# A two-layer hybrid backbone kernel: fill products before TensorE's waits, the routing order, an earlier load of the Fourier matrices, tap norms as columns, and the first low parts moved

## The chip, the cores and the metric

The kernel runs on one NeuronCore of a Trainium2 chip. The metric is the device time of one execution in microseconds (us). The engines are named as in the profile: PE is TensorE's matmul side and PEld its weight loads, DVE is VectorE, ACT is ScalarE, POOL is GpSimd, SP is SyncE, which here only issues DMAs.

## The reference, cut to what matters

Two layers work on 256 latent tokens and 256 context tokens, each of 1024 channels, in float32.

```
for l in range(2):
    h  = modulate(rms_norm(x, norm_mix[l]), shift1, scale1)      # all tokens; l = 1: context for k, v only
    p  = h @ w_in[l]                # columns v, x1, x2 (Hyena), q, kv (attention), f (Fourier), three gates
    ya = attention(q, k, v)         # windowed, sink logits, keys of latents and context
    yf = real(fft2(f))              # per sequence of 256, per group of 128 channels
    yh = hyena(v, x1, x2)           # two long convolutions: DFT, times spectrum, inverse DFT
    # the spectra: taps = mlp(positions) * decay;  k = taps / sum(|taps|) over time, per channel
    x += g1 * ((sum of sigmoid(gate_b) * (y_b @ w_b)) @ w_out)
    h2 = modulate(rms_norm(x, norm_ffn[l]), shift2, scale2)
    aff = sigmoid(h2 @ w_router)    # 16 experts in 4 groups; best group, then its top 2
    x += g2 * sum over the token's 2 experts of weight * (silu(h2 @ Wg) * (h2 @ Wu)) @ Wd
out = rms_norm(x, norm_final)
```

Layer 1 carries on only the latent tokens: it has two blocks of 128 tokens where layer 0 has four.

## The kernel before

**Tiles.** Tokens stand in blocks of 128 (`T`, four in layer 0, two in layer 1). Products are of 128 rows by 512 columns into one of seven PSUM banks that go round (bank 7 is for the modulation). Large float32 products are made of three products of fp32r parts: ACT copies a weight quarter into its high part (`split_high`, L1020, or `high` for experts, L1252), DVE subtracts to get the low part (`split_low`, `low`, L1369), and PE runs high x high, high x low, low x high. Small products and transposes are plain float32.

**Order.** The five engines run five programs written out by hand and joined by semaphores. `plan_jobs(l)` lists every PSUM result of a layer in PE's order with the engine that takes it out ("act" or "dve"); on PE `begin(name)` waits until the bank's former result is taken, and on ACT and DVE `take(name)` waits for the product. Each engine runs strictly in its own order, so an instruction that waits holds up all that stand behind it.

**The opening.** `OPENING` interleaves the first modulation group (eight "units", each a 1 MB load and one set of products) with the making of layer 0's filter spectra in steps 0 to 7 (`filter_step`). Steps 2 and 3 make the taps and their absolute values, steps 4 and 6 the norm (`tap_norm`: PE sums over time with a matrix of ones, DVE takes the reciprocal, L1424), steps 5 and 7 the five spectra of an order (`tap_spectra`: PE, then one DVE multiply by `rnorm` each, L1369). Layer 1's steps run at the end of layer 0, PE's one after the other, DVE's between the two `combine` calls that add the experts' outputs to x.

**The rows.** `first_norm` modulates the rows of a block on DVE (`modulated`, L1495 and L1369), PE transposes them (`turn_row`, L2041), ACT takes the high part, DVE the low part (`low_rows`), and `project` multiplies by v's weights. In layer 0 DVE makes v's four low parts after the second row. Then x1, x2, q, kv and f follow, while SP stores and loads rows for the short convolution that DVE runs (`convolve`).

**Fourier, attention, Hyena.** The Fourier matrices (`four`, 640 KB) are loaded by POOL (L823) after the last convolution of the layer, since they lie where its stage rows lie. PE runs fp and fy (two products each), then attention, then for each order the spectra of u (eight products of 512 columns), DVE's ten multiplies, and the inverse products c behind this wait:

```
for s in range(nt // 2):
    pe.wait_ge(spec_ready, 2 * T_BEFORE[l] + 2 * (o * (nt // 2) + s + 1))
    for tt in range(2):
        b = begin("c", l, o, s, tt)
```

**Routing.** After w_out's products per block come the norm, the transposes of the new rows (hT), and the router products (`logits`: 8 products with 16 columns). ACT copies them, takes high parts of the first expert's first two weight quarters (`high(0, 0)`, `high(0, 1)`) between the last but one and the last block, and applies the sigmoid. DVE ranks (`ranked`), PE counts (`cnt`, `tot`), DVE makes the places of experts 0 and 1, and `place_first` on PE gathers expert 0's rows by products. Then the experts run, 12 weight quarters of 1 MB each.

Of the kernel before, what the change touches and what calls it, by code (L numbers as in the profile page):

```python
# [177 lines left out]
def filter_jobs(l, g):  # L178

    taps = [[("f3", l, o, sign, tt) for sign in (1, 0) for tt in range(2)] for o in range(2)]  # L180
    spec = [[("fk", l, o, b) for b in range(5)] for o in range(2)]
    return [[("fl", l, 1)], [("fl", l, 2)], taps[0], taps[1], [("fn", l, 0)], spec[0], [("fn", l, 1)], spec[1]][g]

# [18 lines left out]
def hybrid_kernel(nc, A, out):  # L202
    jobs = [(("fc",), "dve")]
    for kind, *what in OPENING:
        if kind == "filter":
            jobs += [(n, "dve") for n in filter_jobs(*what)]
    for l in range(DEPTH):
        for g in range(FILTER_STEPS if l else 0):
            jobs += [(n, "dve") for n in filter_jobs(l, g)]
# [49 lines left out]
    with ctx:  # L259
# [58 lines left out]
        rnorm = [mixed[:, 2560:3072], mixed[:, 5120:5632]]  # L318
# [9 lines left out]
        four = work[:, 0:1280]  # L328
# [142 lines left out]
        abs_ready = sem("abs_ready")  # L471
        hid_ready = sem("hid_ready")
# [280 lines left out]
        def _(pool):  # L753
# [65 lines left out]
            for l in range(DEPTH):  # L819
                T = tokens_of(l)  # L820
                Lb = NE * l
                pool.wait_ge(conv_done, 3 * (T_BEFORE[l] + len(T)))
                pool.dma_start(four, A["k_four"]).then_inc(four_loaded, 16)  # L823
# [138 lines left out]
        def _(act):  # L962
# [87 lines left out]
            def filter_step(l, g):  # L1050
# [4 lines left out]
                if g in (2, 3):  # L1055
                    o = g - 2
                    for sign in (1, 0):
                        for tt in range(2):
                            act.wait_ge(dve_took, TAKEN[("f3", l, o, sign, tt)])
                            nc.scalar.activation(filt_abs[l][o][sign][:, tt, :], filt_pm[l][o][:, sign, tt, :], ACT.Abs)\  # L1060
                                .then_inc(diff_abs, 1)

            for kind, *what in OPENING:
                if kind == "filter":
# [4 lines left out]
                    if what == [0, 7]:  # L1069
# [3 lines left out]
            for l in range(DEPTH):  # L1073
# [89 lines left out]
                for s in range(len(T) // 2):  # L1163
                    for g in range(5):
# [3 lines left out]
                        if g > 0:  # L1168
                            b = take(("fy", l, s, g - 1))
                            nc.scalar.activation(yfT[:, g - 1, s * SEQ:(s + 1) * SEQ], b[:, 0:SEQ], ACT.Copy)\  # L1170
# [90 lines left out]
                nc.scalar.activation(rt[:, 0, 0:len(T) * NE], rt[:, 0, 0:len(T) * NE], ACT.Sigmoid).then_inc(aff_ready, 1)  # L1261

# [82 lines left out]
                weigh(l, early_blocks(l), GOT_EARLY[l])  # L1345
# [5 lines left out]
        def _(dve):  # L1351
# [75 lines left out]
            def tap_spectra(l, o):  # L1427
# [1135 lines left out]
```

## Time and profile before

| what | value |
|---|---|
| median of three runs | 2232.47 us (2231.63 to 2233.43) |
| the profiled execution's own time | 2234.48 us |
| its span in the trace | 2232.9 us |
| PE busy | 2072.1 us (93%), 9594 matmuls |
| DVE busy | 1628.2 us (73%) |
| ACT busy | 1162.4 us (52%) |
| mean granted TensorE clock | 0.967 of full |

A granted clock of 1.00 is 2.4 GHz, 0.50 is 1.2 GHz. Every stage has its own bound, so shares of the whole span say little; the chain of waits and the windows of single stretches are to be read.

### The profile page before, as it was taken

The page shows a single profiled execution, that of the slowest core. Times are in us where ns is not written, and L with a number is a line of the kernel's source. Part 1 is how long each engine was busy: PE and PEld are TensorE (multiplying, and loading weights), DVE is VectorE, ACT ScalarE, POOL GpSimd, SP SyncE. Part 2 cuts the span into 40 slices and gives each one's busy share as a digit, 9 for nine tenths or more (in the row PEclk, how much of TensorE's full clock was granted, in tenths as well). Part 3 has the DMA queues.
Part 4 walks back from the last instruction along what each step waited for, and adds up shares of the span by engine and source line. Part 5 has one row for each costly group of instructions (what it writes and reads, how often), then busy time and mean ns, then how long its engine had stood idle before and what let it go on. Part 6 is the DMA issues. An engine that isn't in the chain of part 4 may idle for free.

```text
span 2232.9 us, 26104 instructions
## 1 busy us (share of the span) xinstructions
PE 2072.1 (93%) x9594; PEld 1606.3 (72%) x9594; DVE 1628.2 (73%) x1648; ACT 1162.4 (52%) x1121; POOL 186.8 (8%) x244
## 2 busy tenths in 40 slices
PE   6899999999989999999999797899889999999993
PEld 2687746666777888888887375567678888888882
DVE  4674681233657999999999876545669999999994
ACT  3223602122226777777776344234447777777772
POOL 2000000111003000000000200000110000000001
PEclk9999999999979999999999898999889999999997
DMA  9665006666358999999999566056579999999992
GB/s 343 216 227 203 11 5 226 234 234 223 131 198 294 375 398 388 398 395 386 406 389 385 212 226 238 8 206 227 212 279 373 381 402 394 390 403 387 395 396 106
DMA packets 131134, 630.75 MB, mean 282 GB/s; under 512 B 13677, under 2 KB 15865, under 8 KB 74860
## 3 DMA queue, kind: packets, MB, share of 16 engines
q1 hardware_dynamic: 101432, 505.23, 59.0%
q0 software_dynamic: 26704, 119.69, 14.3%
q10 hardware_dynamic: 2916, 4.73, 0.6%
q8 instruction: 53, 0.87, 0.2%
q14 instruction: 29, 0.24, 0.0%
HBM read 597.39 MB, written 32.20 MB: 282 GB/s over the span
## 4 chain that ended last, share of the span: by engine, by line
PE 82%; DVE 8%; DMA 4%; issue 3%; ACT 2%; SPq 1%; DVEq 0%; POOL 0%; ACTq 0%; POOLq 0%
PE bank L2036 76%; PE bank L2373 3%; DVE work L1369 2%; DVE ring L1369 2%; DMA work<-hp_dram 2%; PE bank L2058 2%; DMA ring<-in_w_mod_dram 1%; PE bank L2246 1%; DVE m_lo L1369 1%; PE bank L2041 1%; DVE mixed L1369 1%; ACT w_hi L1252 1%; DVE w_lo L1369 1%; ACT m_hi L1020 0%; DMA ring<-in_w_in_dram 0%
## 5 line engine op out<-in xcount | busy, mean ns | idle before, releaser
L1369 DVE TENSOR_TENSOR w_lo<-ring,w_hi 128x2048 fp32r<-128x2048 f32 x384 | 873.5, 2288 | 110.5 <-ACT w_hi L1252 110.2
L1252 ACT ACTIVATE w_hi<-ring 128x2048 fp32r<-128x2048 f32 x384 | 737.2, 1921 | 248.3 <-PE bank L2036 248.3
L2036 PE MATMUL bank<-w_hi,xsT_hi 128*128 128x512 f32 x1024 | 399.4, 390 | 6.5 <-DVE xsT_lo L1369 4.7
L2036 PE MATMUL bank<-w_lo,xsT_hi 128*128 128x512 f32 x1024 | 398.5, 389 | 0.0
L2036 PE MATMUL bank<-w_hi,xsT_lo 128*128 128x512 f32 x1024 | 315.3, 389 | 0.0
L1020 ACT ACTIVATE m_hi<-ring 128x1024 fp32r<-128x1024 f32 (+1 forms) x128 | 131.1, 1032 | 349.9 <-PE bank L2036 303.3
L1369 DVE TENSOR_TENSOR m_lo<-ring,m_hi 128x1024 fp32r<-128x1024 f32 (+1 forms) x128 | 150.9, 1190 | 208.4 <-ACT m_hi L1020 206.4
L2036 PE MATMUL bank<-m_hi,hT_hi 128*128 128x512 f32 (+1 forms) x640 | 250.5, 391 | 16.9 <-DVE m_lo L1369 4.8
L2036 PE MATMUL bank<-m_lo,hT_hi 128*128 128x512 f32 (+1 forms) x688 | 263.6, 383 | 0.0
L2036 PEld LDWEIGHTS bank<-w_hi,xsT_hi 128*128 128x128 f32 x1024 | 192.2, 188 | 48.7 <-DVE xsT_lo L1369 5.3
L2036 PE MATMUL bank<-m_hi,hT_lo 128*128 128x512 f32 (+1 forms) x592 | 225.3, 381 | 0.0
L2036 PEld LDWEIGHTS bank<-w_hi,xsT_lo 128*128 128x128 f32 x1024 | 192.2, 188 | 40.0
L2036 PEld LDWEIGHTS bank<-w_lo,xsT_hi 128*128 128x128 f32 x1024 | 192.2, 188 | 39.7
L2036 PE MATMUL bank<-w_hi,hexpT_hi 128*128 128x512 f32 x512 | 203.3, 397 | 5.8 <-issue 5.8
L2036 PE MATMUL bank<-w_lo,hexpT_hi 128*128 128x512 f32 x512 | 200.1, 391 | 0.0
L2036 PEld LDWEIGHTS bank<-m_hi,hT_hi 128*128 128x128 f32 x640 | 122.2, 191 | 65.7 <-issue 25.4
L2036 PE MATMUL bank<-w_hi,hexpT_lo 128*128 128x512 f32 x512 | 158.4, 391 | 0.0
L2036 PEld LDWEIGHTS bank<-m_lo,hT_hi 128*128 128x128 f32 x688 | 131.2, 191 | 23.4
L2036 PEld LDWEIGHTS bank<-m_hi,hT_lo 128*128 128x128 f32 x592 | 112.5, 190 | 21.8
L2036 PEld LDWEIGHTS bank<-w_hi,hexpT_hi 128*128 128x128 f32 x512 | 96.9, 189 | 26.2 <-issue 7.0
L2036 PEld LDWEIGHTS bank<-w_hi,hexpT_lo 128*128 128x128 f32 x512 | 96.4, 188 | 20.9
L2036 PEld LDWEIGHTS bank<-w_lo,hexpT_hi 128*128 128x128 f32 x512 | 96.7, 189 | 19.1
(240 smaller groups left out, 2256.3 us busy)
## 6 DMA issues: line engine op xcount, KB each, us to landing
ring<-in_w_exp_gate_dram SPq DMA_DIRECT2D x128, 1024.0 KB, 8.7
ring<-in_w_exp_up_dram SPq DMA_DIRECT2D x128, 1024.0 KB, 7.3
ring<-in_w_exp_down_dram SPq DMA_DIRECT2D x128, 1024.0 KB, 7.7
ring<-in_w_in_dram SPq DMA_DIRECT2D x44, 1024.0 KB, 5.9
work<-in_w_mod_dram POOLq DMA_DIRECT2D x40, 1024.0 KB, 6.2
ys_dram<-work POOLq DMA_DIRECT2D x32, 512.0 KB, 7.8
work<-hp_dram SPq DMA_DIRECT2D x54, 256.0 KB, 4.4
work<-mod_dram POOLq DMA_DIRECT2D x12, 1024.0 KB, 9.6
```

Of the source, the lines that this page charges most:

```text
L1020: nc.scalar.activation(high_of(key, q)[:, 0:n], ring[:, cols], ACT.Copy).then_inc(split_hi, 1)
L1252: nc.scalar.activation(w_hi[:, pos % N_SPLIT, :], raw(i), ACT.Copy).then_inc(hi_done, 1)
L1369: return nc.vector.tensor_tensor(o, a, b, op)
L2036: return nc.tensor.matmul(o, a, b, start=first, stop=last)
L2041: ins = nc.tensor.transpose(dst[:, j * P:(j + 1) * P], src[:, j * P:(j + 1) * P], ident)
L2058: ins = nc.tensor.matmul(bank[MOD_BANK][32 * j:32 * (j + 1), :], c_act[:, k, :], src[:, j * CH:(j + 1) * CH], start=k == 0, stop=k == KB - ...
L2246: ins = nc.tensor.matmul(b[at_d:at_d + HD, 0:P], vrow[:, k, g * HD:(g + 1) * HD], PT[:, (i - 3) % 2, g, n, :], start=n == 0, stop=n == len ...
L2373: ins = nc.tensor.transpose(dst[:, j * P:(j + 1) * P], s4[:, j // 2, j % 2, :], ident)
```

## The change

- `keep_busy(b, n)` issues n float32 products of the identity with 256 columns of the DFT matrix into a bank that the next job overwrites. It stands before waits of PE: 8 (layer 1: 14) before the first row of the first norm, 4 before v's first product in layer 0, 3 (layer 1: 6) and 2 before the router products of the last two blocks, 1 before the last h2 row, 12 (layer 1: 10) before `cnt`, 1 before `place_first`, and 8 before c in layer 1 alone. `begin` is moved ahead of these waits.
- The sum of absolute taps is made as columns: eight products with one column each, a reciprocal of 128x4, one multiply with the identity (`norm_at`), one product with ones that spreads it back over 512 columns (job "fr", behind the third spectrum), and a copy by ACT into `rnorm`. DVE waits for that copy before the first spectrum's multiply. At the end of layer 0 ACT's two `weigh` calls stand between these copies.
- In layer 0 v's high parts are made right after the first "fr" copy, and v's low parts one by one between the five multiplies of the first spectra.
- The Fourier matrices are loaded to another place after the last row transposes of the first norm, in two DMAs; ACT waits for the last convolution before the first `yfT` write.
- Routing: `high(0, 0)` goes before the last but one router copy, `high(0, 1)` behind the sigmoid; `low(0, 1)` goes behind `idx_tok`; the maximum of `tot` is taken earlier.

```diff
+def filter_taker(name):
+    return "act" if name[0] == "fr" else "dve"
...
+        norm_at = [[filt_abs[l][o][0][:, 0, :].rearrange("p (j n) -> p j n", j=4) for o in range(2)] for l in range(DEPTH)]
+        rcol = [mixed[:, at:at + 8].rearrange("p (o j) -> p o j", o=2) for at in (3300, 5120)]
...
-        four = work[:, 0:1280]
+        four, four_d = work[:, 3072:4096], work[:, 5632:5888]
...
+                pool.wait_ge(mm_done, DONE[("hT", l, 0, 3, 1)])
+                pool.dma_start(four_d, A["k_four"][:, 1024:1280]).then_inc(four_loaded, 16)
+                pool.dma_start(four, A["k_four"][:, 0:1024]).then_inc(four_loaded, 16)
                 pool.wait_ge(conv_done, 3 * (T_BEFORE[l] + len(T)))
-                pool.dma_start(four, A["k_four"]).then_inc(four_loaded, 16)
...
+                if g in (5, 7):
+                    o = g // 7
+                    b = take(("fr", l, o))
+                    nc.scalar.activation(rnorm[l][o], b[:, :], ACT.Copy).then_inc(act_took, 1)
...
-                    if what == [0, 7]:
+                    if what == [0, 5]:
                         for _ in split_high(("in", 0, "v")):
...
+                            if g == 1:
+                                act.wait_ge(conv_done, 3 * (T_BEFORE[l] + len(T)))
                             nc.scalar.activation(yfT[:, g - 1, s * SEQ:(s + 1) * SEQ], b[:, 0:SEQ], ACT.Copy)\
...
+                high(0, 0)
                 logits(l, T[-2])
-                high(0, 0)
-                high(0, 1)
                 transposed(l, T[-1])
                 logits(l, T[-1])
                 act.wait_ge(act_took, TAKEN[("r", l, T[-1])])
                 nc.scalar.activation(rt[:, 0, 0:len(T) * NE], ..., ACT.Sigmoid).then_inc(aff_ready, 1)
+                high(0, 1)
...
-                weigh(l, early_blocks(l), GOT_EARLY[l])
+                for i, tb in enumerate(early_blocks(l)):
+                    weigh(l, [tb], GOT_EARLY[l])
+                    if l + 1 < DEPTH:
+                        filter_step(l + 1, 5 + 2 * i)
...
             def tap_norm(l, o):
                 b = take(("fn", l, o))
-                nc.vector.reciprocal(rnorm[l], b[:, :]).then_inc(dve_took, 1)
+                nc.vector.reciprocal(rcol[l][:, o, :], b[:, 0:4]).then_inc(dve_took, 1)
                 dve.wait_ge(dve_took, took[0])
+                TT(norm_at[l][o], ident.unsqueeze(1).broadcast_to([P, 4, P]),
+                   rcol[l][:, o, :].unsqueeze(2).broadcast_to([P, 4, P]), ALU.mult).then_inc(norm_spread, 1)
+            def tap_spectra(l, o, beside=()):
+                dve.wait_ge(act_took, TAKEN[("fr", l, o)])
                 for k in range(5):
                     b = take(("fk", l, o, k))
-                    TT(made_spectra[l][:, o, k, :], b[:, :], rnorm[l], ALU.mult).then_inc(dve_took, 1)
+                    TT(made_spectra[l][:, o, k, :], b[:, :], rnorm[l][o], ALU.mult).then_inc(dve_took, 1)
                     dve.wait_ge(dve_took, took[0])
+                    for _ in beside:
+                        break
...
-                    filter_step(*what)
+                        tap_spectra(0, 0, split_low(("in", 0, "v")))
+                    else:
+                        filter_step(*what)
...
-                    if l == 0 and tb == 1:
-                        for _ in split_low(("in", 0, "v")):
-                            pass
...
                 low(0, 0)
-                low(0, 1)
                 dve.wait_ge(aff_ready, l + 1)
...
                         .then_inc(idx_ready, 1)
+                low(0, 1)
                 dve.wait_ge(second_mm, l + 1)
...
+            def keep_busy(b, n):
+                for _ in range(n):
+                    mm(b[:, 0:2 * P], ident, dft[:, 0, 0:2, :].rearrange("p b m -> p (b m)"), True, True)
...
-                for tt in range(2):
-                    ins = mm(b[:, :], ones, filt_abs[l][o][1][:, tt, :], tt == 0, tt == 1)
+                for j in range(4):
+                    for tt in range(2):
+                        ins = mm(b[:, j:j + 1], filt_abs[l][o][1][:, tt, j * P:(j + 1) * P], ones[:, 0:1], tt == 0, tt == 1)
...
+                    if k == 3:
+                        pe.wait_ge(norm_spread, 2 * l + o + 1)
+                        b = begin("fr", l, o)
+                        mm(b[:, :], ones, norm_at[l][o].rearrange("p j n -> p (j n)"), True, True).then_inc(mm_done, 1)
...
+                def fill_of(p, k):
+                    if p == 0 and k == 0:
+                        return 14 if l else 8
+                    return int(p == 1 and k == nt - 1)
                 def turn_row(p, k, tb, row):
-                    pe.wait_ge(rows_ready, ROWS_AT[l, p] + k + 1)
                     for half in range(2):
                         b = begin("hT", l, p, tb, half)
+                        if half == 0:
+                            keep_busy(b, fill_of(p, k))
+                            pe.wait_ge(rows_ready, ROWS_AT[l, p] + k + 1)
...
+                        b = begin(*name)
+                        if l == 0 and tb == 0:
+                            keep_busy(b, 4)
                         pe.wait_ge(dve_took, TAKEN[ready(tb)])
-                        b = begin(*name)
...
-                        pe.wait_ge(spec_ready, 2 * T_BEFORE[l] + 2 * (o * (nt // 2) + s + 1))
                         for tt in range(2):
                             b = begin("c", l, o, s, tt)
+                            if tt == 0:
+                                keep_busy(b, 8 if nt == 2 else 0)
+                                pe.wait_ge(spec_ready, 2 * T_BEFORE[l] + 2 * (o * (nt // 2) + s + 1))
...
+                    b = begin("r", l, tb)
+                    if tb in T[-2:]:
+                        keep_busy(b, 2 if tb == T[-1] else 3 if l == 0 else 6)
                     pe.wait_ge(act_took, TAKEN[("hT", l, 1, tb, 1)])
...
+                b = begin("cnt", l)
+                keep_busy(b, 12 if nt == 4 else 10)
                 pe.wait_ge(sel_ready, l + 1)
...
+                    keep_busy(bank[2], 1)
                     pe.wait_ge(placed, 2 * l + 1)
```

## Rows read from the trace of the kernel before

**Rows 1.** Chain of waits, opening: start us, length us, what.

```profile
43.60 19.08 PE bank L2036 x44
...
68.64 4.62 DVE m_lo L1369 x4
...
74.52 7.38 PE bank L2036 x24
...
82.77 5.49 PE bank L2036 x24
```

**Rows 2.** Timeline of DVE, opening and last h2 row: start us, us, instruction, idle before.

```profile
40.56 3.36 DVE L1424 RECIPROCAL mixed<-bank 128x512 f32<-128x512 f32 x1 [1.36 <-PE bank L2036]
...
45.84 0.18 DVE L1450 RECIPROCAL stat<-stat 128x4 f32<-128x4 f32 x1 [0.27 <-ACT stat L1001]
...
62.79 0.69 DVE L1369 TENSOR_TENSOR ring<-bank,mixed 128x512 f32<-128x512 f32 x1 [1.02 <-PE bank L2036]
...
642.88 1.22 DVE L1369 TENSOR_TENSOR mixed<-mixed,work 128x1024 f32<-128x1024 f32 x1
```

**Rows 3.** Timeline of PE: router products and transposes of layer 0, fy of layer 1.

```profile
637.20 1.85 PE L2036 MATMUL bank<-wr,hT 128*128 128x16 f32 x16
638.90 1.07 PE L2041 MATMUL bank<-const,mixed 128*128 128x128 f32 x8
641.66 3.59 PE L2036 MATMUL bank<-wr,hT 128*128 128x16 f32 x16 [1.69 <-ACT hT L1032]
...
1379.05 1.03 PE L2036 MATMUL bank<-ring,work 128*128 128x256 f32 x4
```

**Rows 4.** Chain of waits, routing of layer 0.

```profile
647.18 1.90 ACT w_hi L1252
...
650.10 3.61 PE bank L2036 x16
...
659.32 14.70 PE bank L2036 x88
```

**Rows 5.** Windows there: A:B length, busy PE PEld DVE ACT POOL, clock, DMA, GB/s.

```profile
662.60:669.30 6.70, 6.70 (x36) 6.70 (x35) 3.15 (x14) 0.00 (x0) 0.00 (x0) 0.56 0.00 0
669.30:674.00 4.70, 4.70 (x41) 4.52 (x39) 0.84 (x3) 0.60 (x1) 2.19 (x3) 1.00 0.18 61
```

**Rows 6.** Window before layer 1's first row.

```profile
1274.70:1282.90 8.20, 0.00 (x0) 0.00 (x1) 7.52 (x15) 0.20 (x1) 0.53 (x1) 0.79 0.70 291
```

**Rows 7.** Chain of waits, layer 1's first products.

```profile
1285.35 1.97 PE bank L2041 x8
1287.32 23.00 PE bank L2036 x96
```

**Rows 8.** Windows before and in the Fourier products of layer 1.

```profile
1365.20:1372.60 7.40, 0.00 (x1) 0.00 (x1) 7.02 (x8) 0.68 (x2) 1.58 (x3) 0.71 0.66 254
1372.60:1379.00 6.40, 6.40 (x8) 2.71 (x9) 0.00 (x0) 0.60 (x1) 0.00 (x0) 0.54 0.96 406
```

**Rows 9.** Chain of waits there.

```profile
1368.31 4.24 DMA work<-in_k_four_dram
...
1372.60 14.71 PE bank L2036 x36
```

**Rows 10.** Window between Hyena's spectra and its inverse products, layer 1.

```profile
1429.10:1433.00 3.90, 0.01 (x1) 0.00 (x0) 3.73 (x6) 0.00 (x0) 0.00 (x0) 1.00 0.00 0
```

**Rows 11.** Chain of waits, Hyena's inverse products of both orders, layer 1.

```profile
1433.06 8.84 PE bank L2036 x16
...
1454.55 10.05 PE bank L2036 x16
```

**Rows 12.** Chain of waits, routing of layer 1.

```profile
1619.03 3.61 PE bank L2036 x16
...
1627.22 1.05 PE bank L2036 x4
...
1629.38 6.79 PE bank L2036 x36
```

More of the change, by code:

```diff
@@ L181, in filter_jobs @@
     spec = [[("fk", l, o, b) for b in range(5)] for o in range(2)]
+    for o in range(2):
+        spec[o].insert(3, ("fr", l, o))
     return [[("fl", l, 1)], [("fl", l, 2)], taps[0], taps[1], [("fn", l, 0)], spec[0], [("fn", l, 1)], spec[1]][g]
+def filter_taker(name):
+    return "act" if name[0] == "fr" else "dve"
 FILTER_STEPS = 8
@@ L205, in hybrid_kernel @@
         if kind == "filter":
-            jobs += [(n, "dve") for n in filter_jobs(*what)]
+            jobs += [(n, filter_taker(n)) for n in filter_jobs(*what)]
     for l in range(DEPTH):
         for g in range(FILTER_STEPS if l else 0):
-            jobs += [(n, "dve") for n in filter_jobs(l, g)]
+            jobs += [(n, filter_taker(n)) for n in filter_jobs(l, g)]
         jobs += plan_jobs(l)
@@ L317, in hybrid_kernel @@
         w2 = [mixed[0:64, 2112:2240], work[0:64, 7488:7616]]
-        rnorm = [mixed[:, 2560:3072], mixed[:, 5120:5632]]
+        norm_at = [[filt_abs[l][o][0][:, 0, :].rearrange("p (j n) -> p j n", j=4) for o in range(2)] for l in range(DEPTH)]
+        rnorm = [[filt_abs[0][0][0][:, 1, :], mixed[:, 2560:3072]], [filt_abs[1][o][0][:, 1, :] for o in range(2)]]
+        rcol = [mixed[:, at:at + 8].rearrange("p (o j) -> p o j", o=2) for at in (3300, 5120)]
         zero_i = mixed[:, 2240:2240 + ROWS_PER_PART].bitcast(I32)
@@ L471, in hybrid_kernel @@
         abs_ready = sem("abs_ready")
+        norm_spread = sem("norm_spread")
         hid_ready = sem("hid_ready")
@@ L1864, in _ @@
                        rt1[:, 5 + e, 0:nt].unsqueeze(2).broadcast_to([P, nt, P]), ALU.is_equal).then_inc(placed, 1)
+                b = take(("tot", l))
+                nc.vector.tensor_reduce(most[:, :], b[:, 0:NE], AX.X, ALU.max).then_inc(dve_took, 1)
                 m_over = NE * OVER_BLOCKS[l]
@@ L1884, in _ @@
                         .then_inc(idx_ready, 1)
+                low(0, 1)
                 dve.wait_ge(second_mm, l + 1)
                 nc.vector.tensor_copy(idx_over[:, 0:1], bank[MOD_BANK][:, 0:1]).then_inc(second_idx, 1)
-                b = take(("tot", l))
-                nc.vector.tensor_reduce(most[:, :], b[:, 0:NE], AX.X, ALU.max).then_inc(dve_took, 1)
                 def shares():
@@ L2196, in _ @@
                     turn(b, qrow[:, tb, :], 4).then_inc(mm_done, 1)
-                pe.wait_ge(four_loaded, 16 * (l + 1))
+                pe.wait_ge(four_loaded, 32 * (l + 1))
                 pe.wait_ge(act_took, TAKEN[("in", l, "f", T[-1])])
@@ L2211, in _ @@
                             for j in range(2):
-                                ins = mm(b[:, 0:SEQ], four[:, 1024 + j * P:1024 + (j + 1) * P],
+                                ins = mm(b[:, 0:SEQ], four_d[:, j * P:(j + 1) * P],
                                          pq[:, (g - 1) % 2, j * SEQ:(j + 1) * SEQ], j == 0, j == 1)
@@ L2300, in logits @@
                 def logits(tb):
+                    b = begin("r", l, tb)
+                    if tb in T[-2:]:
+                        keep_busy(b, 2 if tb == T[-1] else 3 if l == 0 else 6)
                     pe.wait_ge(act_took, TAKEN[("hT", l, 1, tb, 1)])
-                    b = begin("r", l, tb)
                     for k in range(KB):
@@ L2322, in _ @@
                 mm(b[:, 0:P], ones, tri, True, True).then_inc(mm_done, 1)
+                b = begin("cnt", l)
+                keep_busy(b, 12 if nt == 4 else 10)
                 pe.wait_ge(sel_ready, l + 1)
-                b = begin("cnt", l)
                 sel = rt[:, 9, :]
```

1 line of the change is left out of this document (removed).

## The prediction

> **What bounds the kernel now.** I read the totals, then the chain of waits from end to end, then the stretches of it in which PE stands still or runs at half clock, with windows and timelines. PE is busy 93% of the span and the chain is mostly PE: time can come off only in three ways, a pause of PE that ends earlier, products that run at full clock instead of half, or products taken away. The reader is to see six such places: the opening up to v's first products [rows 1, 2], the routing of layer 0 [rows 3 to 5], the first norm of layer 1 [rows 6, 7], its Fourier products [rows 8, 9], its Hyena inverse products [rows 10, 11], and its routing [rows 12]. In the routing the same eight router products take 1.85 us at 637.20 and 3.59 at 641.66 [rows 3]: between them PE did eight transposes and stood still for 1.69. So half clock is there after a small pause, when only small products went before.
>
> **The fills.** One fill is a float32 product of 256 columns. Four records, that is two products, take 1.03 at 1379.05 [rows 3], which makes 0.43 to 0.5 each at full clock; half the price of a 512-column one at half clock (19.08 for 22, 0.87 each [rows 1]) gives the same 0.43, and that stretch is at full clock. At half clock a fill takes 0.87. Layer 0 has 8+4+3+1+2+12+1 = 31, layer 1 14+16+6+1+2+10+1 = 50, in all 81: 35 us at full clock, 70 at half. The pauses that they stand in add up, stretch by stretch as below, to some 34. So at full clock they fit within about 1 us; at half clock they don't. No row has a fill at its place, so the price is bounded by these two; I take full clock, since PE comes to nearly all of them out of dense products.
>
> **Opening, +3.6.** PE is the bound from 43.60 for 19.08, to 62.68. Two "fr" products join (2 x 0.87 = 1.7, PE ends at 64.4). The norm as eight one-column products has no row; the nearest are the eight router products (1.85 [rows 3]) and the two 512-column ones it replaces (1.73): nothing. The wide reciprocal of 3.36 becomes 0.18 and a multiply of 0.69 [rows 2], but DVE is not last here. The last spectrum's multiply ends at 65.1 instead of 63.5, so the rows come 1.5 later. Then the block of four low parts, 4.62 [rows 1], is gone from between the second row and its low rows: it now lies between multiplies that wait for PE anyway (cover: PE's ten products there; without it, 4.6 comes back). Low rows start at 68.64 + 1.5 = 70.1, end at 71.4; with the second row's transposes and four fills (1.7) v starts at 72.8, not 74.52: 1.7. Its first 24 products take 7.38 at half clock, the next 24 take 5.49 [rows 1]: 1.9 more. Bounds: -1.7 (only the added products show) to 6.5 (4.62 and 1.9 whole).
>
> **Routing of layer 0, +9.4.** PE comes to the router products of the third block at 641.66; at full clock they end at 643.5, not 645.3. ACT's high part of 1.90 stood before the last transposes' copies [rows 4]; it now lies ahead of the third copy, where ACT waits. The last row is ready when DVE ends at 644.10 [rows 2]. Transposes 1.07, copies 1.1, eight products 1.85: 648.2, where the chain has 650.10 + 3.61 = 653.7 [rows 4]. Ranking stays at 659.32 - 653.71 = 5.6, and twelve fills (5.2) lie in it. From `cnt` on the chain has 14.70: 6.70 at a clock of 0.56 becomes 3.7, 4.70 is at 1.00 already [rows 5], and the 3.3 before becomes some 2.3. So expert 0's rows stand at 653.8 + 10.7 = 664.5 instead of 674.0; I take 9.4. `low(0, 1)` (half of DVE's two, about 2.3) moves behind the indices and is hidden until 665. If the small products lose the clock in spite of fills, 4 to 5 is left: bounds 4 and 9.8.
>
> **First norm of layer 1, +3.3.** DVE is last before it: 2 x 3.36 goes, 2 x 0.87 comes [rows 2]. But PE has only 8.20 of standing still before the first row [rows 6] and gets two products of 0.87 for "fr", and ACT's two copies wait behind `weigh`, so I take 1.7 of the 5.0 for the rows. Fourteen fills (6.1) fit in what is left. Transposes of 1.97 become 1.07 [rows 7, 3], v's 96 products of 23.00 become 4 x 5.49 = 22.0 [rows 7, 1]; 0.3 is lost to fills that end behind the row. Bounds: 1.7 (the clock alone is not won) to 6.8 (DVE's 5.0 whole).
>
> **Fourier, +10.4, in layer 1 alone.** PE stands still for 7.40 before fy [rows 8]; the load that ends it takes 4.24 and was issued only at the end of the last convolution [rows 9]. It now comes 40 us earlier. Next late is DVE, busy for 7.02 of those 7.40 [rows 8] with low parts that attention wants, but PE's fy and fp lie before that: 36 records, 14.71 [rows 9], of which 6.40 at 0.54 [rows 8] becomes 3.4. ACT's new wait for the last convolution is met 2 us before its first copy; behind it would stand all copies that attention needs. The 640 KB now run beside the loads of weights and of convolution rows, where DMA is busy: from 0 to the load's own 4.24 if a convolution load waits for all of it; I take 1.0. Bounds 5 and 11.5. Layer 0 has no such pause: nothing.
>
> **Hyena c, layer 1, +5.0.** PE stands still for 3.90 [rows 10] while DVE multiplies. Sixteen records of 512 columns take 8.84 and 10.05 [rows 11]; at full clock 8 x 0.87 = 6.9 each. Eight fills (3.4) fit in 3.90. Bounds: -1 (half clock in the fills) to 5.0.
>
> **Routing of layer 1, +8.2.** As in layer 0: 3.61 at 1619.03 [rows 12], and as much for the block before; the last router products end 5.5 earlier, `cnt` (1.05) saves 0.5, and the first half of the gathering, 6.79 [rows 12], goes at the rate of the full-clock one (4.70 for 41 [rows 5]) to some 4.1 to 4.6: 2.2. Bounds 4 and 8.7.
>
> The experts, attention, w_out and the tail are untouched. Sum: 3.6 + 9.4 + 3.3 + 10.4 + 5.0 + 8.2 = 39.9. From it I take 1.0 for the moved load and 2.9 because the clock will not hold in every one of the ten stretches: 36. The profiled execution took 2234.48, so 2198.5 in its terms; the median of the runs is 2.0 less: 2232.5 - 36 = 2196.5.
>
> **A rule weighed.** The row: the router products fall to half clock after a pause of only 1.69 [rows 3]. The Trainium skill ("TensorE: Matmul & The Clock Gate", section "HAM oscillation — how this bites in real kernels") puts such falls down to waits for data between bursts of matmuls. By that rule alone the five or six fills before router products buy nothing, and the small products can't lose the clock again once a burst went before; by the row they may. The trace differs from the rule at 641.66 and so gives the first rival its chance.
>
> **Rivals.**
> *The clock falls all the same.* The 16-column router products, transposes and 32-column counts keep PE little occupied, fills or not. For it: the 3.59 after 1.69 of pause [rows 3], and 0.56 over 6.70 of uninterrupted small products [rows 5]. Against: 1.00 right behind, on products of the same kind [rows 5]. Everywhere: 0 + 5 + 1.7 + 9.5 + 0 + 4 = 20, so 2212. In the two routings alone: 4.4 + 4.2 less, 31, so 2201. Chance 0.20, mostly of the second form.
> *The Fourier load is not free.* It takes queue and memory while rows for the convolutions come in, and the conv chain ends later; or PE waits at another place in the same stretch. For it: DMA at 0.66 to 0.96 there [rows 8]. Against: at the new place it has 40 us to land. About 5 lost: 2201. Chance 0.10.
> *The fills run at half clock (the other side).* 81 x 0.87 = 70 in 34 of pauses is 36 over. What doesn't hang on the clock is some 15.5: 3 in the opening, 1.7 in the norm, 7.4 in the Fourier pause, 2 x 1.7 of order in the routings. Result 2232.5 + 36 - 15.5 = 2253; slower as soon as the overshoot passes 15.5, that is when over 45% of the fills' time is at half. For it: fills in a pause that follows small products, twelve before `cnt`. Against: full-clock rows of the same form [rows 3] come right behind others. Chance 0.03.
> *The change doesn't do what it says:* the fills' bank is not free in time, `begin` now standing ahead of the waits, and PE stops at `begin` instead. The time is that of the first rival, and its chance is in it.
>
> **How the numbers follow.** 0.67 for the forecast, whose own range is 2190 to 2202 (sum 39.9 and a little, down to 31). The rivals reach to 2212; leaving out 2 in 10 on both sides together gives 2189 to 2209. A difference under 0.2% (4.5 us) can't be told from none here. Slower needs the third rival: 0.03. Within 0.2% needs two rivals together: 0.02. Faster: 0.95.
>
> **What would show it.** After the change: v's first 24 products 5.5 long and starting near 72.8; all router sets 1.85; `cnt` near 650 (654 less the opening's shift); no 4.24 DMA in the chain before fy, and a clock near 1.00 there; c twice at 6.9. Wrong: fills of 0.87 in a row, router sets of 3.6 behind fills, a new wait on DVE before attention, or a window before layer 1's convolutions longer than before.

## The result, and the profile after the change

| | median us | ratio to before, 95% interval |
|---|---|---|
| before | 2232.95 (4 runs, 2231.63 to 2238.47) | |
| changed | 2205.39 (4 runs, 2201.41 to 2210.15) | 0.9873 [0.9843, 0.9902] |

The change takes 27.6 us off, where 36 were forecast. Repeated twice beside later experiments it took off 28.6 (2207.17 against 2235.78) and 24.4 (2211.66 against 2236.08). Its runs lie 8.7 apart, those of before 6.8, and the quick ones have the higher mean granted clock: 2201.41 at 0.984, 2208.69 at 0.979. The medians below are those of all runs; beside them stood one execution of experiment 5 (2654.83 us at a granted clock of 0.765) and one of the kernel before beside experiment 12 (3881.42 at 0.794), which move a median by less than 0.5.

The profiled execution took 2202.1 us with a span of 2200.5, 32.4 below the span of before; it is one of the two quicker of the four. Lines differ by the change: L2036 of before is L2061 here, L2041 is L2071, L1369 is L1390. First the chain of waits (start, length, what), from the opening to the experts of layer 0, then in layer 1 from the first norm to Hyena:

```profile
43.29 17.45 PE bank L2061 x52
...
70.37 1.06 PE bank L2071 x8
71.44 7.20 PE bank L2061 x32
78.63 0.87 PE bank L2071 x8
79.51 5.46 PE bank L2061 x24
...
644.85 2.74 PE bank L2061 x20
...
653.20 11.12 PE bank L2061 x90
...
1276.38 1.06 PE bank L2071 x8
1277.59 22.06 PE bank L2061 x96
...
1354.57 11.52 PE bank L2061 x36
...
1410.24 7.15 PE bank L2061 x16
...
1430.04 7.15 PE bank L2061 x16
```

Against [rows 1] v's second set starts at 79.51, 3.26 earlier. Against [rows 4, 5] the last router set with its fills takes 2.74 in place of 3.61, `cnt` starts at 653.20 and the gathering takes 11.12 in place of 14.70. Against [rows 7] layer 1's v takes 22.06, not 23.00; against [rows 8, 9] no load stands before fy any more and 36 records take 11.52, not 14.71; against [rows 11] c takes 7.15 twice, not 8.84 and 10.05.

Windows of the same run (A:B, length, then PE, PEld, DVE, ACT, POOL busy with instructions, granted clock, DMA, GB/s) show where the clock held and where not:

```profile
175.85:179.90 4.05, 4.05 (x12) 3.19 (x13) 3.88 (x7) 1.69 (x6) 0.53 (x1) 0.64 1.06 407
...
648.00:653.20 5.20, 5.08 (x25) 4.13 (x23) 4.57 (x17) 1.89 (x2) 0.00 (x0) 1.00 0.97 368
653.20:664.30 11.10, 11.10 (x90) 10.59 (x90) 7.39 (x23) 0.60 (x1) 1.60 (x2) 1.00 0.62 241
1268.80:1276.40 7.60, 7.08 (x38) 6.10 (x36) 7.02 (x13) 1.86 (x4) 0.53 (x1) 1.00 0.42 177
...
1354.57:1360.00 5.43, 5.43 (x17) 2.70 (x16) 5.29 (x7) 2.27 (x5) 1.05 (x2) 1.00 0.61 191
...
1583.30:1586.70 3.40, 3.40 (x15) 2.97 (x15) 2.64 (x3) 2.46 (x4) 0.57 (x1) 0.50 1.01 420
1596.90:1600.40 3.50, 3.50 (x20) 3.50 (x18) 2.47 (x4) 0.49 (x1) 0.00 (x0) 0.51 0.77 309
```

Layer 0's routing is at 1.00 throughout and layer 1's is twice at half clock (1583 and 1597). F's products in layer 0 fall to it within their first 4.05 us (0.64, from 175.85 on).

What each stage gained, from the PE timelines: how much earlier than in the run of before the stage's last mark comes, less what was won up to its first mark. Each column is one profiled execution, and these stand differently to the medians of their kernels: changed and changed again are 3 under them, no fills 5.7 over, fills only 2.4 over, the third profile of the change (experiment 1) 2.9 over. "Last version" is experiment 12. The forecast's stages sum to 39.9, of which it took off 3.9.

| stage | forecast | changed | changed again | changed, third | no fills | fills only | Fourier only | last version |
|---|---|---|---|---|---|---|---|---|
| to v's first product | 1.7 | 1.7 | 0.5 | -0.7 | -2.2 | -0.1 | -0.1 | 1.2 |
| v to third router set | 1.9 | -1.3 | -2.8 | -1.5 | -2.0 | -1.6 | -0.7 | 0.4 |
| routing, layer 0 | 9.4 | 9.3 | 9.3 | 4.9 | 4.2 | 4.0 | 0.0 | 8.6 |
| experts, layer 0 | 0 | -1.7 | 0.0 | -3.8 | -2.3 | -1.1 | 0.0 | -2.1 |
| layer 1 up to kv | 3.3 | 2.6 | 2.9 | 2.6 | 2.5 | -0.2 | 1.3 | 4.5 |
| kv to c (Fourier, attention) | 10.4 | 12.2 | 10.7 | 12.2 | 10.7 | 0.2 | 12.2 | 12.1 |
| c to first router set | 5.0 | 6.2 | 5.5 | 3.6 | 0.1 | 3.2 | 0.0 | 5.4 |
| routing, layer 1 | 8.2 | 4.7 | 4.4 | 5.9 | 2.8 | 3.2 | 0.1 | 7.9 |
| experts, tail | 0 | -1.3 | -0.1 | -3.4 | -1.2 | -1.2 | -0.7 | 0.3 |
| span | 36 | 32.4 | 30.4 | 19.9 | 12.5 | 6.4 | 12.1 | 38.3 |

Two rows of this table need a second look. V's first product came 1.7 earlier than before in one profile of the change, 0.5 earlier in the next and 0.7 later in the third. In the third PE was below full clock where the first and the kernel before are at 1.00, around and behind the new one-column products:

```profile
38.00:44.00 6.00, 4.87 (x40) 2.38 (x40) 1.90 (x4) 5.74 (x10) 0.00 (x0) 0.91 1.01 406
44.00:50.00 6.00, 6.00 (x19) 2.38 (x12) 2.39 (x8) 0.20 (x1) 2.02 (x4) 0.81 1.05 386
```

The same is in experiments 2, 7, 8 and 9 and in none of the three profiles without the norm as columns (before, 3, 4). And the last down products of layer 0's experts begin behind the same pause of 2.92 in the first two profiles of the change, but only the second keeps the clock; that is nearly all of the -1.7 (first, then second):

```profile
1216.67:1229.50 12.83, 12.79 (x48) 10.07 (x48) 6.95 (x9) 2.74 (x3) 0.54 (x1) 0.87 0.40 139
1219.37:1230.50 11.13, 11.13 (x48) 8.90 (x48) 6.94 (x9) 2.33 (x2) 0.54 (x1) 1.00 0.46 161
```

### The profile page after: what moved, and what is told of

The parts are those of the page before. It is cut to its first block, busy times and chain, and to the rows that moved or that the text cites. A ratio compares the mean times of both kernels' runs of the same rounds, so it can differ in the third digit from the quotient of the medians.

```text
span 2200.5 us, 26546 instructions
## 1 busy us (share of the span) xinstructions
PE 2089.0 (95%) x9812; PEld 1626.4 (74%) x9812; DVE 1617.6 (74%) x1652; ACT 1163.9 (53%) x1125; POOL 188.3 (9%) x246
## 4 chain that ended last, share of the span: by engine, by line
PE 83%; DVE 7%; DMA 4%; issue 2%; ACT 2%; SPq 1%; DVEq 0%; POOL 0%; ACTq 0%; POOLq 0%
PE bank L2061 77%; PE bank L2423 3%; DVE work L1390 2%; DVE ring L1390 2%; DMA work<-hp_dram 2%; PE bank L2088 2%; DMA ring<-in_w_mod_dram 1%; PE bank L2071 1%; PE bank L2290 1%; DVE m_lo L1390 1%; ACT m_hi L1032 0%; DVE w_lo L1390 0%; DMA ring<-in_w_in_dram 0%; SPq L656 0%; DVE mixed L1390 0%
## 5 line engine op out<-in xcount | busy, mean ns | idle before, releaser
L1390 DVE TENSOR_TENSOR w_lo<-ring,w_hi 128x2048 fp32r<-128x2048 f32 x384 | 873.5, 2288 | 108.1 <-ACT w_hi L1270 107.9
L2061 PE MATMUL bank<-w_hi,xsT_hi 128*128 128x512 f32 x1024 | 399.4, 390 | 6.5 <-DVE xsT_lo L1390 6.1
L2061 PE MATMUL bank<-w_lo,xsT_hi 128*128 128x512 f32 x1024 | 398.5, 389 | 0.0
L2061 PE MATMUL bank<-w_hi,xsT_lo 128*128 128x512 f32 x1024 | 315.3, 389 | 0.0
L1390 DVE TENSOR_TENSOR m_lo<-ring,m_hi 128x1024 fp32r<-128x1024 f32 (+1 forms) x128 | 151.0, 1190 | 210.1 <-ACT m_hi L1032 208.3
L2061 PE MATMUL bank<-m_lo,hT_hi 128*128 128x512 f32 (+1 forms) x688 | 263.4, 383 | 0.0
L2061 PE MATMUL bank<-m_hi,hT_hi 128*128 128x512 f32 (+1 forms) x640 | 249.8, 390 | 12.6 <-ACT ring L1223 4.1
L2061 PEld LDWEIGHTS bank<-w_hi,xsT_hi 128*128 128x128 f32 x1024 | 192.2, 188 | 48.8 <-DVE xsT_lo L1390 6.9
L2061 PE MATMUL bank<-m_hi,hT_lo 128*128 128x512 f32 (+1 forms) x592 | 226.0, 382 | 0.0
L2061 PEld LDWEIGHTS bank<-w_hi,xsT_lo 128*128 128x128 f32 x1024 | 192.2, 188 | 40.0
L2061 PEld LDWEIGHTS bank<-w_lo,xsT_hi 128*128 128x128 f32 x1024 | 192.2, 188 | 39.6
L2061 PE MATMUL bank<-w_hi,hexpT_hi 128*128 128x512 f32 x512 | 204.6, 400 | 5.8 <-issue 5.8
L2061 PE MATMUL bank<-w_lo,hexpT_hi 128*128 128x512 f32 x512 | 201.4, 393 | 0.0
L2061 PEld LDWEIGHTS bank<-m_hi,hT_hi 128*128 128x128 f32 x640 | 122.4, 191 | 60.8 <-issue 26.9
L2061 PE MATMUL bank<-w_hi,hexpT_lo 128*128 128x512 f32 x512 | 159.4, 393 | 0.0
L2061 PEld LDWEIGHTS bank<-m_lo,hT_hi 128*128 128x128 f32 x688 | 131.2, 191 | 23.5
L2061 PEld LDWEIGHTS bank<-m_hi,hT_lo 128*128 128x128 f32 x592 | 112.8, 191 | 21.4
L2061 PEld LDWEIGHTS bank<-w_hi,hexpT_hi 128*128 128x128 f32 x512 | 97.8, 191 | 26.5 <-issue 7.0
L2061 PEld LDWEIGHTS bank<-w_hi,hexpT_lo 128*128 128x128 f32 x512 | 97.0, 189 | 21.1
L2061 PEld LDWEIGHTS bank<-w_lo,hexpT_hi 128*128 128x128 f32 x512 | 97.4, 190 | 19.4
```

The lines of the kernel that those rows point to most:

```text
L1390: return nc.vector.tensor_tensor(o, a, b, op)
L2061: return nc.tensor.matmul(o, a, b, start=first, stop=last)
```

## The experiments

My theory A at first: the mechanisms are as forecast, some of the clock is not held, and the opening's gain is given back before layer 0's routing. Its rivals are in the expectations.

**1. The change again, three times in all (e1, e11).** No edit.

> The changed kernel once more, unaltered, as the measure for the rest. Theory A (what is lost between 2196 and 2205 is half-clock time that comes and goes with the run): times spread over 2200 to 2211 and go with the mean clock, about 1.1 us for each 0.0005 of it; PE at half clock again in or near the routing of layer 1. Rival B (the loss is fixed work, such as fills that overshoot): the spread is under 2 us, as before the change.

Measured 2207.17 (2204.21 to 2208.56), 28.6 off; clock 0.980 to 0.985. The quickest run has 0.985, the slowest two 0.981 and 0.980: the spread goes with the clock, so fixed work alone doesn't make it. It is some 0.5 us per 0.0005 (4.35 between 0.985 and 0.981), half of what I gave, and the spread was smaller too.

> The changed kernel unaltered, as the measure for this call. Theory A: 28 to 29 below the kernel before, with 23 us or more for f's products in layer 0. Rival (the first two profiles were chance): f's products at 21.7.

Measured 2211.66 (2202.82 to 2214.56), 24.4 off: below what I expected. f's products again took over 23, as in the two earlier profiles of the change. New in its profile is half clock in layer 0's routing. Its PE timeline (in brackets idle time before, and who ended it) and its window there:

```profile
643.83 1.96 PE L2061 MATMUL bank<-wr,hT 128*128 128x16 f32 x16 [0.40 <-ACT hT L1044]
...
649.18 3.43 PE L2061 MATMUL bank<-wr,hT 128*128 128x16 f32 x16
```

```profile
647.00:657.30 10.30, 10.30 (x37) 9.03 (x36) 6.03 (x14) 3.49 (x7) 0.12 (x1) 0.50 1.01 394
```

A pause of 0.40 among router products and transposes is the only one near, and some 3 us behind it PE falls to half clock for 10.30; the first profile has the same pause (0.39) and no fall. So whether the pause or the small products themselves lose the clock here isn't shown. The stage gained 4.9, not 9.3.

**2. No fills (e2).**

```diff
-                for _ in range(n):
+                for _ in range(0):
```

> The changed kernel without any of its 81 fills, all else kept. Theory A: what is left is what does not hang on the clock, 7.4 in the Fourier pause, 1.7 in layer 1's norm and 3.4 from the routing's order, 12.5 in all: about 2220, with router sets of 3.6 and 14.7-like gatherings back. Rival B (the fills cost about what they give): within 2 us of the changed kernel, 2203 to 2207.

Measured 2216.24 (2211.91 to 2221.94), ratio 0.9903 [0.9888, 0.9918]: 19.5 off, so the fills bring 9.1 of the 28.6. I had expected 12.5 without them and 16 from them. In its profile the Fourier part gives 10.7, not 7.4, and the two routings 7.0, not 3.4: part of what I put down to the fills comes without them. The chain of waits of this run in layer 0's routing:

```profile
645.88 2.71 PE bank L2061 x16
648.59 1.80 PE bank L2071 x8
651.15 3.58 PE bank L2061 x16
660.43 13.64 PE bank L2061 x88
```

The router set of 3.58 at half clock is back and the gathering takes 13.64. The new order alone still gives 4.2 there.

**3. Fills only (e3).** The kernel before with `keep_busy` at the 81 places.

> The kernel before with the 81 fills alone. Theory A: the clock's part of the sum, 17 to 20 less some overshoot: 2214 to 2219. Rival B: 2230 to 2236. A second rival (the fills need the new order to fit in the pauses, and overshoot without it): over 2222, with the last rows waiting behind fills.

Measured 2225.77 (2220.10 to 2228.88), 0.9948 [0.9932, 0.9964]: 10.0 off. It lies in the second rival's region, but one place speaks against its overshoot: before layer 1's first row the 14 fills end 2.16 too early, and the transposes behind take 1.92, half clock. In the routings the fills alone bring 4.0 and 3.2, with the order 9.3 and 4.7. What is missing against 17 to 20 is in the table: nothing in layer 1 up to kv, 3.2 instead of 5 around c, a loss of 1.6 before layer 0's routing, and the experts' rows.

**4. Fourier matrices only (e4).** The earlier load and ACT's wait in the kernel before.

> The kernel before with the Fourier matrices' earlier load and ACT's wait alone. Theory A: the 7.4 pause goes and the products after it keep full clock, at least 7.4 and up to 10.4 off: 2222 to 2225, with no pause before fy in layer 1. Rival C (the moved 640 KB delay the convolution rows): under 5 off, 2228 or more, and a conv chain that ends later than 1367.

Measured 2222.01 (2219.82 to 2226.28), 0.9935 [0.992, 0.995]: 13.8 off, the largest part of the change. Its windows ahead of and in the Fourier products of layer 1:

```profile
1359.00:1363.32 4.32, 3.33 (x15) 2.29 (x13) 4.08 (x14) 2.88 (x4) 0.00 (x0) 1.00 0.47 156
1364.75:1376.30 11.55, 11.55 (x38) 6.34 (x39) 7.36 (x10) 5.31 (x11) 1.57 (x3) 1.00 0.80 310
```

Where [rows 8] has a pause of 7.40 and a clock of 0.54 behind it, PE works at 1.00 without a single fill: taking the pause away kept the clock as well.

**5. Norm as columns and low parts only (e5).** The changed kernel with the fills, the Fourier move and the routing's order taken back.

> The change without fills, without the Fourier move and with the old routing order: only the norm as columns, ACT's fr copies, the moved low parts of v, and the earlier maximum of tot that the shifted banks need. Theory A (the opening's gain is given back by transfers before layer 0's q products; layer 1's norm gives 1 to 2): 2233 to 2236 where before gives 2235.8, v's first product 0 to 2 us earlier or later, the third router set of layer 0 not earlier. Rival (the opening was sized rightly and fills or the Fourier load spoil it): 3 to 6 off, 2230 to 2233, and the shift is still there at the third router set.

Measured 2230.35 against 2233.90, 0.9980 [0.9971, 0.9989]: 3.6 off, within the rival's 3 to 6 and above theory A's; the interval (2.5 to 6.5) reaches to both. It has no profile to read, so whether the gain lies in the opening or in layer 1's norm stays open. The parts come to 13.8 + 9.1 + 3.6 = 26.5 of 28.6. The 2.1 that is left for the routing's order is within their noise, and the profile without fills gives the order more (4.2 and 2.8), so this split isn't sharp.

**6. Layer 0's Fourier load late again (e6).**

```diff
-                pool.wait_ge(mm_done, DONE[("hT", l, 0, 3, 1)])
+                if l:
+                    pool.wait_ge(mm_done, DONE[("hT", l, 0, 3, 1)])
+                else:
+                    pool.wait_ge(conv_done, 3 * (T_BEFORE[l] + len(T)))
```

> The changed kernel with layer 0's Fourier matrices loaded after its last convolution again, layer 1's as changed. Theory A (640 KB beside layer 0's convolution rows cost about 1 us and bring nothing there): 1 to 2 off the changed kernel, 2205 to 2206, with shorter row loads between 97 and 165. Rival (the convolution rows are late for another reason): within 0.5 of it.

Measured 2203.82, 30.1 off, 0.9862 [0.9839, 0.9885]. Its runs spread over 14 and the interval overlaps the changed kernel's: the 1.5 between it and the 28.6 can't be told from nothing.

**7. More cover in the routings (e7).**

```diff
-                        keep_busy(b, 2 if tb == T[-1] else 3 if l == 0 else 6)
+                        keep_busy(b, 2 if tb == T[-1] else 4 if l == 0 else 8)
...
+                keep_busy(bank[MOD_BANK], 3)
                 for i in (2, 3):
...
-                    keep_busy(bank[2], 1)
...
+                    if e == 0:
+                        b = take(("tot", l))
+                        nc.vector.tensor_reduce(most[:, :], b[:, 0:NE], AX.X, ALU.max).then_inc(dve_took, 1)
```

> The changed kernel with more cover in the routings: 4 (layer 0) and 8 (layer 1) fills before the last but one router set, 3 fills into the modulation's bank between tot and the gathering in place of the one, and the maximum of tot taken between the two place tables. Theory A (layer 1's routing loses the clock at the 0.76 pause behind its six fills and at the 1.20 before the gathering): 2 to 4 off, 2203 to 2205, the gathering 0.5 earlier, no stretch at half clock. Rival (three fills too many delay the gathering and the clock falls anyway): 0 to 2 more.

Measured 2204.90, 29.0 off, 0.9857 [0.9838, 0.9875]: in the whole time no more than the change. The traces do tell them apart. The PE timeline of the changed kernel in layer 1's routing, then of this one:

```profile
1578.09 2.76 PE L2061 MATMUL bank<-const 128*128 128x256 f32 x12
1581.61 2.08 PE L2061 MATMUL bank<-wr,hT 128*128 128x16 f32 x16 [0.76 <-ACT hT L1044]
...
1584.52 1.91 PE L2071 MATMUL bank<-const,work 128*128 128x128 f32 x8
...
1596.04 0.70 PE L2061 MATMUL bank<-const 128*128 128x256 f32 x2 [1.20 <-DVE most L1891]
1596.57 3.30 PE L2061 MATMUL bank<-mixed,work 128*128 128x128 f32 x16
```

```profile
1591.34 1.09 PE L2072 MATMUL bank<-const,work 128*128 128x128 f32 x8
...
1600.63 1.54 PE L2062 MATMUL bank<-const 128*128 128x256 f32 x6
1602.01 2.04 PE L2062 MATMUL bank<-mixed,work 128*128 128x128 f32 x16
```

In the changed kernel six fills end 0.76 early and the eight transposes behind take 1.91 at half clock, not 1.09. Then PE waits 1.20 for `most`, DVE's maximum of `tot`, and the one fill stands behind that wait where it covers nothing: the first half of the gathering takes 3.30, not 2.04. With the cover the routing of layer 1 gains 7.9 (forecast 8.2), and again 7.9 in experiments 10 and 12, against 4.4 to 5.9 in the profiles of the change and of experiments 6, 8 and 9. In layer 0 the added cover costs 0.7 (8.6, not 9.3). The total shows neither: this run lost 2.3 to 3 more between c and the first router set than the first two profiles of the change, and it was at half clock there from 1557.9 to 1564.7.

**8. A later v (e8).** 14 fills in place of 8 before the first row, 12 in place of 4 before v.

> The changed kernel with 14 fills instead of 8 before the first row and 12 instead of 4 before v's first product: v starts up to 6 us later. Theory A (between v and q layer 0 waits for transfers that don't start later for it): under 3 us more, the delay shrinking between 75 and 180. Rival (the opening's time goes to the end whole): 5 to 6 more, 2212 to 2213.

Measured 2211.89, 22.0 off, 2.4 to 6.6 less than the three measurements of the change; the intervals overlap, so the time alone doesn't decide. The profiles do: v starts at 79.18, which is 4.0 to 6.4 later than in the three profiles of the change, and the third router set comes 6.3 to 9.0 later. A delay made in the opening does not shrink up to there, and theory A's account of it falls.

**9. Fills before f (e9).** F's products are the next for which PE waits after v. In the changed kernel they begin behind a wider pause (2.29, before 1.66), and the clock falls behind it: 23.68 for 96 products, not 22.05. I put the wider pause down to the earlier v. The first product of f in the profiles before and changed, of experiment 3 (v at 74.63, as before) and of experiment 8 (v at 79.18, the latest of all) shows that this was wrong:

```profile
178.47 0.47 PE L2036 MATMUL bank<-m_hi,hT_hi 128*128 128x512 f32 x1 [1.66 <-ACT mixed L1144]
...
175.85 0.47 PE L2061 MATMUL bank<-m_hi,hT_hi 128*128 128x512 f32 x1 [2.29 <-ACT mixed L1160]
...
177.89 0.47 PE L2036 MATMUL bank<-m_hi,hT_hi 128*128 128x512 f32 x1 [2.58 <-ACT mixed L1144]
...
183.52 0.77 PE L2061 MATMUL bank<-m_hi,hT_hi 128*128 128x512 f32 x1 [3.62 <-ACT mixed L1160]
```

```diff
                         banks = [begin(*n) for n in names]
+                        keep_busy(banks[0], {("in", 0, "f"): 5}.get(key, 0))
```

> The changed kernel with 5 more fills in layer 0, ahead of f's products, in the pause that grew from 1.66 to between 2.2 and 3.8 when v started earlier. Theory A (the opening's gain is lost half as waiting there and 1.7 to 2.7 as half clock behind it): f's 96 products take 21.7 and not 23.3 or more, 1.5 to 2.5 off the changed kernel of the same call. Rival (that half clock is chance and the fills delay f): within 1 of it, f's products as long as before.

Measured 2207.00 (0.9869 [0.9849, 0.9890]), 29.1 off, 4.7 under the 2211.66 measured beside it, with overlapping intervals. In the rows the saving was missed: from v's first product to f's last takes 2.4 longer than there. The PE timeline:

```profile
178.78 4.08 PE L2061 MATMUL bank<-const 128*128 128x256 f32 x10 [3.29 <-ACT mixed L1160]
182.52 0.58 PE L2061 MATMUL bank<-m_hi,hT_hi 128*128 128x512 f32 x1
```

The pause stands ahead of the fills, which then run at half clock and delay f by 3.7. PE waits in `begin` for a bank with kv's results. ACT frees it late; its timeline in the changed kernel:

```profile
174.20 1.06 ACT L1032 ACTIVATE m_hi<-ring 128x1024 fp32r<-128x1024 f32 x1 [0.61 <-DMA ring<-in_w_in_dram]
175.17 0.26 ACT L1159 ACTIVATE work<-bank 128x128 f32<-128x128 f32 x1
175.32 0.27 ACT L1160 ACTIVATE mixed<-bank 128x128 f32<-128x128 f32 x1
```

Before the copies of kv stands the third high part of f, which waits for its weights' load. That load does move with v: it starts 93.4 behind v's first product before and 93.1 in the changed kernel, and lands at 176.81 and 174.18. What doesn't move it is v at full clock, which ends kv's products 100.7 behind v's first, not 102.3. How long the load takes (8.1 to 10.0 in the profiles with this order) widens or narrows the pause as well.

**10. Fills in other pauses (e10).** Experiments 6, 7 and 9 together, and fills before layer 1's kv (4) and taps (9), layer 0's second gate products (5) and the merged rows' transposes (2, 3; layer 1: 5, 3).

> The late first load and the routing's fills of the two runs before, f's 5 fills, and fills in the other pauses that half clock follows in the changed kernel: 4 before layer 1's kv, 5 before layer 0's second gate products, 2 and 3 (layer 1: 5 and 3) before the first transposes of merged rows, 9 before layer 1's taps. Theory A (each pause of 1.5 to 3 costs 1.7 to 3.4 of half clock behind it): 8 to 14 off the changed kernel, 2193 to 2199 where before gives 2235, mean clock 0.988 or more. Rival (other pauses fall into the clock's windows instead): under 4 off.

Measured 2205.42 (2199.53 to 2207.26), 0.9858 [0.9837, 0.9879], 30.7 off and 6.2 under the change measured beside it: neither 8 to 14 nor under 4. The clock rose to 0.988 as expected; the third router set came at 650.0, 6.2 later than in the changed kernel measured beside it (643.8). F's products end 3.0 later, behind fills that stand behind `begin`; the rest lies between f and the third router set.

**11. kv's copies first (e12).** The version of experiment 10 without the gate's fills, and on ACT:

```diff
                 ahead = split_high(("in", l, "f"))
-                for _ in range(3):
+                for _ in range(3 if l else 2):
                     next(ahead)
                 for tb in range(4):
                     b = take(("in", l, "kv", tb))
```

> The version with more fills, with one step of ACT's order changed in layer 0 (the four copies of kv's results before the third of f's high parts, which waits for its weights) and without the fills before the second gate products. Theory A': in the run with f's fills the pause of 3.29 came before them, so PE waited for kv's banks, which ACT frees only behind a part that waits for a load. With the copies first the fills stand in the pause: f's products start no later than in the unaltered change against v's last (about 96.5 behind it) and take 21.7 to 22; at the third router set 3 to 6 us are won back against the version with more fills, in all 2196 to 2202 where before gives 2234 to 2236. Rival (the load of f's weights itself is the bound there): f's products start as late as with more fills, 2204 or more.

Measured 2197.38 (2196.26 to 2198.84) against 2236.02, ratio 0.9833 [0.9819, 0.9847]: 38.6 off, the lowest of all. Its interval lies clear of that of e1 (0.9870 [0.9852, 0.9887]), of e11 (0.9883 [0.9862, 0.9904]) and of e9, and overlaps at its upper end those of the first result, of e6, e7 and e10. Against experiment 10 the third router set comes 9.9 earlier, more than the 3 to 6 expected; two things were changed there, the copies and the gate's fills, and what each brought isn't separated. Its PE timeline and window at f:

```profile
175.27 2.40 PE L2065 MATMUL bank<-const 128*128 128x256 f32 x10 [1.19 <-ACT mixed L1163]
177.31 0.58 PE L2065 MATMUL bank<-m_hi,hT_hi 128*128 128x512 f32 x1
```

```profile
177.30:181.00 3.70, 3.70 (x18) 3.07 (x17) 3.56 (x7) 0.72 (x1) 1.60 (x3) 1.00 1.05 403
```

PE stands still for only 1.19, the fills take 0.48 each and f runs at 1.00. F itself starts no earlier, 104.0 behind v's first product (103.0 to 104.6 in the three profiles of the change): the copies' place lets the fills cover the wait, and what is won is the clock. From v to the third router set this is the only run as quick as before (566.8 against 567.2, 568.5 in the changed kernel); experiment 6, with the late Fourier load alone, takes 568.0. The routings of this run, layer 0's and layer 1's:

```profile
636.00:664.00 28.00, 27.66 (x196) 25.08 (x195) 19.08 (x51) 9.73 (x17) 3.42 (x5) 1.00 0.85 331
1576.00:1598.50 22.50, 22.04 (x144) 19.39 (x142) 16.21 (x45) 9.85 (x16) 1.79 (x3) 1.00 1.01 414
```

## Why the prediction was right, and what was mis-sized

The time lies inside the wide range of 2189 to 2209, near its upper end, and outside the forecast's own 2190 to 2202; it is 8.9 above the 2196.5 forecast, and the gain of 27.6 is 8.4 under the 36. The two repeats (28.6 and 24.4) stand the same way. The Fourier, Hyena and layer 0 routing mechanisms are in the traces as worked out; the opening's and layer 1's routing are not. By its steps:

- **Fills.** Price right: 28 records (14 fills) take 6.21 at 1268.79, 0.44 each. What they bring was mis-sized. The text left 15.5 to what doesn't hang on the clock and so 20 to the clock; measured are 19.5 without fills, and 9.1 (experiment 2) or 10.0 (experiment 3) from them. Part of it is only bookkeeping: the Fourier pause gave its clock back without fills.
- **Opening, 3.6.** v came 1.7 earlier in the first profile and its second set 3.26 earlier, as worked out; that the 1.7 fits so well is luck, since the two other profiles have 0.5 earlier and 0.7 later. Of the 3.26, 0.4 was left at the third router set. The pause before f took 0.6 and half clock behind it 1.6, which leaves 1.0 at f's end. That loss doesn't hang on an early v: f's products take over 23 in every profile with the fills or the new norm, but for the three with fills before f (experiments 9, 10 and 12: 22.0, 22.8 and 22.0). Experiment 8 shows that transfers don't absorb a shift. Why the pause is wider with the change isn't shown beyond the two parts named in experiment 9.
- **Routing of layer 0, 9.4.** 9.3 in two profiles, 4.9 in the third; 4.2 comes without fills (one profile), the rest with them, if the clock holds.
- **First norm of layer 1, 3.3.** 2.6, 2.9 and 2.6. v's products 22.06 (forecast 22.0).
- **Fourier, 10.4.** 12.2, 10.7 and 12.2; alone, 12.2 in the profile and 13.8 in the time. The term missed what comes behind: attention's first 36 records take 5.09, not 6.71, in the first profile and alone.
- **Hyena c, 5.0.** 6.2 in the first profile: 4.6 in c itself, where 7.15 stands for the 6.9 worked out, and 1.6 behind it. The other profiles have 5.5 and 3.6.
- **Routing of layer 1, 8.2.** 4.7, 4.4 and 5.9: this is the step that failed. "As in layer 0" did not hold: the pause there is 0.76 longer than six fills, and a wait was overlooked. The four `fr` jobs that were added by then shift the round of seven banks, so that in layer 1 `tot`'s result lies in bank 2 (before: 5), which the gathering needs, and PE waits for DVE's `most` (1.20). Experiment 7 gave 7.9 once both were covered.
- **1.0 for the moved load, 2.9 for the clock.** Experiment 6 can't tell the first from nothing. The second was too small: half clock in f's products (1.6) and in the experts' last down products (1.7) alone come to 3.3 in the first profile, both in stages that the sum left at 0 or in v's.

Of the rivals, the first had part of the truth: the clock falls in layer 1's routing in every profile of the change, and in layer 0's in one of three. The measured time lies between its two forms (2201 and 2212).

The rule weighed in the prediction (the Trainium skill, "TensorE: Matmul & The Clock Gate", section "HAM oscillation — how this bites in real kernels", which puts the falls down to waits between bursts) came out better than I gave it: with its pauses covered the last version ran its router sets, transposes and gatherings at 1.00 in both layers. Nor does it follow from the rule that fills before router products buy nothing: where waits cost the clock, filling them is what should help. But the pauses here are small, 0.40 at 643.83 in one run and 2.29 before f, and behind the same pause of 2.92 the clock is lost in one run (0.87) and kept in another (1.00).

Open: why the experts of layer 0 take 2 us more in the runs without fills and of the last version, whose last down products keep the clock (11.16 and 11.12); and what decides, run by run, which pauses lose the clock.

## What to carry to other kernels

A fill only covers a pause that begins behind it: look up what ends the pause, because a bank wait stands ahead of fills written into that bank. A gain made far ahead of the next wait must be followed to that wait; here 2.2 of 3.26 were lost in and behind the pause before f. Jobs added to a round of banks move the later results to other banks, so look up which result lies where a later step writes. A single profile can flatter a step: v's 1.7 was not there in the third. And taking a pause away was worth the clock behind it too.

## What the runs showed of the hardware

The kernels with the higher mean granted clock are the quicker ones: before 0.963 to 0.968 and 2231 to 2243 us, changed 0.976 to 0.985 and 2201 to 2215, the last version 0.988 to 0.990 and 2196 to 2199. Half clock follows pauses of 0.4 to 2.9 us in one run and not in the next: behind 2.92 before the last down products of layer 0's experts 12.83 at 0.87 in one profile, 11.13 at 1.00 in another. It cost 1.6 us in f's products (23.68 against 22.05), and in the third profile it lasted 10.30. So half clock behind a pause may cost more than the pause: 1.6 behind f's, which had grown by 0.6. Small products need not lose the clock: 90 of them run back to back at 1.00 for 11.10 us in layer 0's routing.
